# Split activations laid out 2192 bytes apart per block of 128 rows instead of 2176, in a two-layer decoder trunk in float32

## What is computed

```python
for i in range(2):
    x = x + 0.5 * swiglu_ffn(rms_norm(x, g_pre[i]), w_gate[i, 0], w_up[i, 0], w_down[i, 0])
    h = rms_norm(x, g_mix[i])
    x = x + (conv_module(h, ...) if i == 0 else gla_mixer(h, ...))
    x = x + 0.5 * swiglu_ffn(rms_norm(x, g_post[i]), w_gate[i, 1], w_up[i, 1], w_down[i, 1])
y = rms_norm(x, g_final)

def swiglu_ffn(h, w_gate, w_up, w_down):
    return (silu(h @ w_gate) * (h @ w_up)) @ w_down
```

## Time and profile before

| | |
|---|---|
| median of 3 runs | 2222.72 us (2222.65 to 2222.73) |
| the profiled execution | 2222.79 us |
| its span, first to last instruction | 2221.1 us |
| mean granted clock of TensorE | 0.987 |
| TensorE busy | 2161.8 us, 97% |
| VectorE, ScalarE, GpSimd busy | 1017.2, 671.1, 136.0 us |

### The profile page before, as it was taken

How to read it: one execution, slowest core, us unless ns; L and a number is a source line. 1 busy time by engine, 2 the same in 40 slices (tenths; PEclk the granted TensorE clock), 3 DMA queues, 4 the chain that set the end, 5 groups by cost and what they waited for, 6 DMA issues and landing times.

```text
span 2221.1 us, 39216 instructions
## 1 busy us (share of the span) xinstructions
PE 2161.8 (97%) x16249; PEld 2074.1 (93%) x16249; DVE 1017.2 (46%) x1303; ACT 671.1 (30%) x1024; POOL 136.0 (6%) x133
## 2 busy tenths in 40 slices
PE   8999999899979999999999999999999899999997
PEld 8999999877769999999999999999987799999997
DVE  4444433288956444433254443233455464444322
ACT  5222222343333322222232222222332242222222
POOL 0000001100003000002100000121000030000000
PEclk9999999999989999999999999999999999999999
DMA  4322223311103322322233322332224133332321
GB/s 141 92 85 85 83 88 88 97 58 39 58 5 90 101 85 85 89 84 86 83 95 90 90 85 81 88 97 77 67 58 136 64 95 95 89 90 85 95 79 67
DMA packets 338763, 185.65 MB, mean 84 GB/s; under 512 B 6013, under 2 KB 334943, under 8 KB 338669
## 3 DMA queue, kind: packets, MB, share of 16 engines
q1 hardware_dynamic: 335228, 172.78, 26.6%
q0 software_dynamic: 3200, 11.64, 1.6%
q10 hardware_dynamic: 256, 0.10, 0.0%
HBM read 177.29 MB, written 8.05 MB: 83 GB/s over the span
## 4 chain that ended last, share of the span: by engine, by line
PE 92%; DVE 3%; issue 2%; ACT 2%; DMA 1%; POOL 0%; ACTq 0%; SPq 0%; DVEq 0%
PE ps L421 80%; PE ps L886 4%; PE ps L442 4%; ACT w_hi L401 1%; PE ps L893 1%; PE ps L1069 1%; PE ps L1075 0%; DMA hist_in<-in_state_conv 0%; DMA pin<-in_gla_onorm_g 0%; PE ps L1008 0%; PE ps L1016 0%; DVE x L1461 0%; DVE x L1667 0%; PE ps L982 0%; DVE ta L1649 0%
## 5 line engine op out<-in xcount | busy, mean ns | idle before, releaser
L421 PE MATMUL ps<-xg_hi,w_hi 128*128 128x272 f32 x3344 | 697.3, 290 | 3.6 <-DVE tb L1409 1.6
L421 PE MATMUL ps<-xg_hi,w_lo 128*128 128x272 f32 x3344 | 693.4, 289 | 0.0
L421 PE MATMUL ps<-xg_lo,w_hi 128*128 128x272 f32 x3344 | 691.1, 288 | 0.0
L401 ACT ACTIVATE w_hi<-raw 128x1024 fp32r<-128x1024 f32 x329 | 348.3, 1059 | 1024.5 <-PE ps L421 974.3
L408 DVE TENSOR_TENSOR w_lo<-raw,w_hi 128x1024 fp32r<-128x1024 f32 x329 | 414.7, 1263 | 443.5 <-ACT w_hi L401 443.0
L421 PEld LDWEIGHTS ps<-xg_hi,w_hi 128*128 128x128 f32 x3344 | 528.2, 189 | 7.0 <-issue 2.5
L421 PEld LDWEIGHTS ps<-xg_lo,w_hi 128*128 128x128 f32 x3344 | 527.2, 189 | 0.0
L421 PEld LDWEIGHTS ps<-xg_hi,w_lo 128*128 128x128 f32 x3344 | 523.5, 189 | 0.0
L421 PE MATMUL ps<-h_hi,w_hi 128*128 128x272 f32 x1536 | 318.3, 288 | 1.6 <-DVE x L1461 0.9
L421 PE MATMUL ps<-h_hi,w_lo 128*128 128x272 f32 x1536 | 317.9, 288 | 0.0
L421 PE MATMUL ps<-h_lo,w_hi 128*128 128x272 f32 x1536 | 316.6, 288 | 0.0
(11 more groups left out here) (258 smaller groups left out, 1296.0 us busy)
## 6 DMA issues: line engine op xcount, KB each, us to landing
raw<-in_ffn_w_gate SPq DMA_DIRECT2D x88, 512.0 KB, 3.8
raw<-in_ffn_w_up SPq DMA_DIRECT2D x88, 512.0 KB, 3.8
raw<-in_ffn_w_down SPq DMA_DIRECT2D x64, 512.0 KB, 4.0
raw<-in_gla_w_in SPq DMA_DIRECT2D x25, 512.0 KB, 3.8
raw<-in_ffn_w_down SPq DMA_DIRECT2D x32, 384.0 KB, 3.4
raw<-in_conv_w_pw SPq DMA_DIRECT2D x24, 512.0 KB, 4.2
raw<-in_gla_w_out SPq DMA_DIRECT2D x8, 512.0 KB, 4.0
st<-in_state_gla POOLq DMA_DIRECT2D x4, 1024.0 KB, 9.4
```

The costliest lines, as they stand in the source:

```text
L401: nc.scalar.activation(w_hi[:, n % RING], raw[:, n % RAW], ACT.Copy).then_inc(w_high, 1)
L421: last = nc.tensor.matmul(ps[:, 2 * pair + c, 0:HALF], w[:, r, k, :], a[:, k0 + k, c * HALF:(c + 1) * HALF], start=(k0 + k == 0 and w is w ...
```

## The change

The tensors xg_hi and xg_lo are allocated with rows of T + 4 = 548 elements instead of 544, and used through a view of the first 544. A block k of them starts 2192 x k bytes behind the first one instead of 2176 x k. The four elements at the end of each row are never read or written. Each of the two tensors becomes 128 bytes longer, so xg_lo starts 128 bytes further on, and h_hi and everything behind it 256 bytes. The tensors that are laid over XG keep their addresses.

```diff
         x = sb("x", [P, M, T])
         XG = taken[0]
-        xg_hi = sb("xg_hi", [P, M, T], F32R)
-        xg_lo = sb("xg_lo", [P, M, T], F32R)
+        XG_STEP = T + 4
+        xg_hi = sb("xg_hi", [P, M, XG_STEP], F32R)[:, :, 0:T]
+        xg_lo = sb("xg_lo", [P, M, XG_STEP], F32R)[:, :, 0:T]
         HHI = taken[0]
```

## The result

The changed kernel takes 2231.04 us in the median of 8 runs (2227.00 to 2231.65), the kernel before 2222.79 (2222.65 to 2223.84): ratio 1.0033, 95% interval 1.0024 to 1.0042. It is slower by 8.25 us. The forecast was 2222.7; the time lies within the range of 2216 to 2243, but it is not "the same", which had the chance of 0.69.

The account below looks back on a forecast made before the run. TensorE's matmuls, mostly at L421, were taken as the bound. Span 2221.1 us plus three terms of 0 and 1.7 us around it gave 2222.8; with the runs' median of 2222.72 the forecast was 2222.7, range 2216 to 2243.

Parts of the forecast that it names:

- the same: Whole kernel: time within 0.2%, 4.4 us, of the kernel before; chance 0.69.
- What bounds the kernel: TensorE, busy 2161.8 of 2221.1 us; 80% of the chain that ended last is the matmul at L421.
- No instruction is added: Whole kernel: no instruction, wait, DMA or byte computed is added or removed by the change.
- Part 2: ScalarE's and VectorE's writes of xg: at most +-10 ns each, 0.08 us at four stage starts, taken as 0.
- Part 1: 10,416 matmuls streaming xg: start phase costs between -12.0 and +7.4 ns each, taken as 0.
- the flaw: Tap matmuls at L886, used as evidence, stream at half L421's rate, so they can hide an extra fetch.
- Part 3: Everything moved by 256 bytes: slower transfers or conversions hide behind TensorE's 6.0 us slots; taken as 0.
- Rival slower: Matmuls on xg wait for aligned fetches: 32-byte pieces cost 19 us (2242), 64-byte 58 us (2280); chance 0.19.
- Rival faster: Matmuls on xg: stream stops hitting the weight load's part of SBUF, gaining at most 94 us (2129); chance 0.10.
- What would show it: Stretches of matmuls: unchanged if right; if wrong, those on xg lengthen or shorten while those on h stay at 16.54 us.

Follow-up runs that it names:

- e3: The change with x padded to the same 2192 bytes as well, so one register serves both tensors; 2224.80 us, ratio 1.0008.
- e1: The change with padding of 16 elements instead of 4, so blocks of xg lie 2240 bytes apart; 2226.81 us, ratio 1.0015.
- g2: The change with GpSimd's additions held back until VectorE's write of xg_lo, in two stages also the next w_lo; 2225.62 us, ratio 1.0011.
- f1: The kernel before with 256 unused bytes between xg_lo and h_hi; 2222.84 us, ratio 0.9998.
- k1: The kernel before with 64 unused bytes ahead of w_hi, moving both weight rings; 2217.92 us in one run, timed again 2218.18 us, ratio 0.9978.
- k2: The kernel before with 64 unused bytes between w_hi and w_lo; 2237.46 us, one run.
- e2c: The kernel before with all of h starting 48 bytes past a multiple of 64, xg still on one; 2225.46 us, ratio 1.0009.
- h1: The kernel before with x, xg, h and rs starting 48 bytes past a multiple of 128, each tensor 64 bytes longer; 2217.97 us, ratio 0.9978.
- f4: The kernel before with 128 unused bytes between xg_hi and xg_lo and 128 behind xg_lo; 2222.25 us, one run.
- g1: The kernel before with GpSimd's additions held back until VectorE's write of xg_lo, in two stages also the next w_lo; 2223.47 us, ratio 1.0000.

## Why the prediction was wrong, point by point

- *What bounds the kernel*: held. The matmuls of L421 are the bound, and hand-overs fill the rest.
- *"No instruction is added"*: this is the step that failed first. 34 more are executed, since x and xg no longer share a stride (the same padding on x takes them away, e3). The diff shows it: the same block index m, held in a loop register, selects a block of x and one of xg in one instruction.
- *Part 2, the writers, +-10 ns each*: failed, and this is the term that cost most. I took it as 0, bounded by the phase of the addresses, which indeed costs nothing (e3), and not by the GpSimd addition that runs beside each write and excludes it. The row had it: xg_lo 771/785/1939. The maximum, 2.5 times the median, says that this instruction sometimes loses something (2 of 48 here), and that needs a rival of its own: what if it always does? The median went to 1918 ns, with 31 of 48 slow. Its price, 1.8 us at one hand-over with 1.3 at the clock behind it and 0.7 at the next, was 4 to 6 us (e1, g2) instead of my 0.08 at most.
- *Part 1, 0 per matmul*: mis-sized. It is +0.27 ns (13 ns a slot, 2.9 us in all), within the bounds of -12.0 and +7.4. The nearest rows, plain f32 taps, couldn't show it, and the flaw was stated.
- *Part 3, 256 bytes*: right as it stood (f1), though 64 bytes there would have been worth -5 or +14 us (k1, k2). The cover I named, a slot's 6 us, hides transfers and conversions, but not a change in the spacing of the matmuls.
- *Rival slower, larger fetch pieces*: right side, wrong mechanism. h at phase 48 got faster (e2c), and with all blocks at 48 everything did (h1).
- *Rival faster, a clash between stream and weight load*: the place of the weight rings does count (k1, k2), and I gave the rival 0.10. The effect goes both ways, and in this change it is on the losing side; that it is a clash isn't shown. My argument against it, that 64 bytes of phase make no difference now, compared stretches that all have the same mixture.
- *What would show it*: the signs were useful. Stretches on xg grew and those on h didn't, and by far less than a fetch piece.

What stays open: what relation of high part, low part and the two rings sets the level, and why f4 and k1 have different levels for the same addresses. Of the 1.4 us in the GLA stage, 1.1 lie in one stretch, from one slot on xg to a later one: 69.47 us (1552.25 to 1621.72) at a granted clock of 0.90 in the change, 68.35 (1546.32 to 1614.67) at 0.93 in the kernel before. The two profiled executions of k1, one and the same kernel, differ as much there (68.16 us at 0.92, 69.47 at 0.90), so this part need not belong to the change; why the clock differs is open. About 2.5 us of the 8.25 are in neither e1 nor e3. That the time of the change is spread over 4.6 us fits the clock: its fastest run, 2227.00, has a mean of 0.988, the others 0.984 to 0.986.

## What to carry to other kernels

Where a diff changes a stride or an offset, compare it with the other operands that the same loop index selects: a shared address computation is a hidden asset, and 0.11 us on one engine went with another winner at a shared port. Read the maximum beside the median: here a maximum at 2.5 times the median, reached by few of the 48, was the sign of a race that was otherwise won. And if matmuls with weight loads fill the time, the relative position of stream and weights is worth a few runs, since it couldn't be argued from the profile here.

## What the runs showed of the hardware

- VectorE with two inputs in SBUF and GpSimd's addition exclude each other: 0.79 and 1.90 us in one order, 1.93 and 1.35 in the other. Held back by a wait, the addition takes 1.36 (g1).
- A float32r matmul of 272 columns with its own load of 128x128 is spaced 124.5 to 126.1 ns on average at 2.4 GHz, by where operands and weights lie (k1 and k2, first pieces); 64 bytes between the two rings make 14 us of 2223 (k2, one run).
- TensorE was idle for 2.36 us ahead of the post-FFN's last block in the changed kernel (released by xg_lo), and had a granted clock of 0.58 in the 3.9 us from 711.00 on; with 0.56 us idle at the same place in the kernel before, it stayed at 1.00.
